# Four experts for each of 32 tokens in a gather, four column groups of TensorE, and a ring of four slots

## The chip, the cores and the metric

The kernel runs on one core of a Trainium2 chip. The metric is the time of one execution on the device, in microseconds (us); lower is better. TensorE is written PE here, its weight loads PEld, VectorE DVE, ScalarE ACT, GpSimd POOL and SyncE SP. A name with a q behind it (POOLq) is an engine's sequencer. "Line 1757" or L1757 is a line of the kernel before; lines of the changed kernel are called so.

## What is computed

One step of a decoder layer: two mixers (an S5 scan and a Mamba-2 scan), a residual, and a channel mixer of single-neuron experts (PEER). The change touches the channel mixer alone. For each of 1088 tokens (1024 of a prompt, 64 sampled) it chooses 8 x 16 = 128 of 16384 experts, and adds up their value rows, each with the gelu of its key row's product with the token:

```python
def peer_ffn(h, w_q, sub_keys, u_tab, v_tab):
    q = (xt @ w_q).astype(F32).reshape(T, PEER_HEADS, 2, PEER_HALF)
    s = jnp.einsum('thid,hikd->thik', q, sub_keys.astype(F32))
    sv, si = lax.top_k(s, PEER_TOPK)
    cand = sv[:, :, 0, :, None] + sv[:, :, 1, None, :]
    cv, cpos = lax.top_k(cand.reshape(T, PEER_HEADS, PEER_TOPK * PEER_TOPK), PEER_TOPK)
...
    idx = i1 * PEER_N_KEYS + i2
    g = jax.nn.softmax(cv, axis=-1)
...
        u = u_tab[ib]
        act = jax.nn.gelu(jnp.einsum('thkd,td->thk', u, xb).astype(F32))
        v = v_tab[ib]
        return jnp.einsum('thk,thkd->td', (gb * act).astype(v.dtype), v)
```

The input xb is the token after an RMSNorm; the sum is added to the residual x, and a last RMSNorm gives the output y. All is 32-bit float, and a row of u or v has 1024 elements. In the kernel's table `uv` the two rows of an expert stand side by side, so one row of it has 8 KB.

## The kernel before

The function `route_and_experts` is the last stage. It works on nine tiles of tokens: eight main tiles of 128 tokens, one turn each of a hardware loop (`Fori(0, MAIN_TILES)`, on every engine), and a last tile of the 64 sampled tokens, written out behind the loop. Within a turn everything is unrolled.

**Gathers.** A main tile has 128 gathers, one for each of a token's 128 experts: gather g brings, for each of the 128 tokens (one to a partition), the row `uv` of its g-th expert, so 128 rows of 8 KB. POOL issues it as one indirect DMA (line 1576) into one slot of `ring`, which has RING = 8 slots. It may do so when the slot's last user is through: `group_done`, raised by PE. The sample tile folds its 64 tokens over 128 partitions (`folded`, three small DMAs), two experts at a time, and has 64 gathers.

**One gather's work** runs through four engines:

- DVE (line 1757) multiplies the u half of the slot by the token rows `h_now` and sums along the row: one dot product for each partition.
- ACT (line 1617) takes the gelu of the 128 dot products.
- DVE (line 1745, `weigh`) makes `diag`, a 128x128 diagonal matrix of gelu times gate. It stands one gather late in DVE's order: behind the dot product of g comes weigh(g - 1).
- PE (line 1832) multiplies `diag` by the v half of the slot, as two matmuls of 512 columns, each of which is two passes in the trace (four records a gather, since the data is fp32), and adds into the PSUM tensor `acc`. Its last matmul raises `group_done`, and POOL issues gather g + 8 into the slot.

**Routing** of the next tile is done meanwhile, in 64 steps (ROUTE_STEPS), one behind every second gather (EVERY = 2), on ACT, DVE and PE, in an order written out by hand: the norm of x, transposes of h (line 1793), the query matmuls (16 steps, line 1803, 16 records each), scores (line 1813), top-k steps on DVE (lines 1658 to 1731, some of them over 2048 elements a partition: lines 1640 and 1722), and a softmax. `index` and `gate` are its results. POOL copies the index to `index_now` (lines 1565 and 1580).

**The end of a tile.** Behind the last gather PE adds x (line 1819); ACT sums the squares (line 1621), loads a function table and takes the root (line 1623), and copies x to `x_now`; DVE takes the reciprocal (line 1766) and writes `out` (line 1768); SP stores it (line 1536) and loads the next x (line 1532). Then every engine branches back to the loop's top, where DVE copies `gate_now` and `h_now` (lines 1749 and 1750) before its first dot product. PE's first `add_x` waits for `x_now` and for `out`.

## Time and profile before

| | us |
|---|---|
| three runs | 4724.04, 4724.33, 4729.05 |
| median | 4724.33 |
| span of the profiled execution | 4728.8 |
| busy in it: PE, DVE, POOL, ACT | 3724.3, 2737.7, 1485.7, 691.1 |
| bytes moved by the gathers' queue | 1140.92 MB |

The last stage starts its gathers at about 1891 us and runs to the end, so it holds six tenths of the time, and all that the change touches. The busy shares of the whole span (PE 79%, DVE 58%, POOL 31%, ACT 15%) mix it with the stages ahead of it and are of little use; the stage is read by windows, by the distance of repeated instructions, and by the chain of waits.

### The profile page before, as it was taken

How to read it: one execution, taken by the hardware profiler on the slowest of the kernel's cores; microseconds unless marked ns; L12 is line 12 of the kernel's file. 1: busy time of each engine (PE TensorE's matmuls, PEld its weight loads, DVE VectorE, ACT ScalarE, POOL GpSimd, SP SyncE). 2: the span in 40 equal slices, each digit the busy share in tenths (PEclk: the TensorE clock that was granted, in tenths of full speed). 3: DMA queues.
4: the chain of work that ended last, by engine and by line, in shares of the span. 5: the costliest groups of instructions: out<-in, count | busy, mean ns of one | idle time of the engine just before them, and what ended most of it. 6: DMA issues, size and time to landing. Idle time of an engine off the chain costs nothing.

```text
span 4728.8 us, 44920 instructions
## 1 busy us (share of the span) xinstructions
PE 3724.3 (79%) x12914; PEld 1960.8 (41%) x12914; DVE 2737.7 (58%) x5963; ACT 691.1 (15%) x1844; POOL 1485.7 (31%) x1547
## 2 busy tenths in 40 slices
PE   8999590745469994887977978978878879779777
PEld 5767460723334443432532523534424325325221
DVE  1000529158831114687686785785886876867865
ACT  1110120112223220101101111111111011011110
POOL 3000310401100000444444443454444444444442
PEclk9999755867679997999999999999999999999999
DMA  4111300121131112999999999999999999999998
GB/s 161 61 40 36 75 2 2 47 95 41 34 152 67 54 44 105 411 412 395 413 418 390 415 419 393 412 421 394 416 419 394 416 413 392 415 389 414 420 401 360
DMA packets 253462, 1271.34 MB, mean 269 GB/s; under 512 B 62096, under 2 KB 92432, under 8 KB 113168
## 3 DMA queue, kind: packets, MB, share of 16 engines
q0 software_dynamic: 156672, 1140.92, 58.6%
q1 hardware_dynamic: 96576, 127.93, 8.1%
q8 instruction: 90, 1.47, 0.1%
q14 instruction: 124, 1.02, 0.1%
HBM read 1226.22 MB, written 40.09 MB: 268 GB/s over the span
## 4 chain that ended last, share of the span: by engine, by line
DMA 23%; PE 21%; DVE 8%; issue 7%; POOL 2%; ACT 0%; POOLq 0%; DVEq 0%; SPq 0%; ACTq 0%
DMA pe_ring<-in_uv,pe_index_now 20%; PE pe_acc L1832 15%; PE pe_ps_q L1803 5%; DVE pe_ring L1757 2%; DMA pe_ring<-in_uv,pe_index 2%; POOL pe_ring L1576 2%; DVE pe_work_a L1640 2%; DVE pe_diag L1745 1%; DVE pe_picked L1722 1%; PE pe_ps_s L1813 1%; PE pe_acc L1819 0%; DMA pe_w_q<-in_w_q 0%; DVE pe_top L1699 0%; ACT pe_square L1621 0%; DVE pe_dot L1757 0%
## 5 line engine op out<-in xcount | busy, mean ns | idle before, releaser
L1832 PE MATMUL pe_acc<-pe_ring,pe_diag 128*128 128x512 f32 (+1 forms) x4352 | 2069.4, 618 | 451.7 <-DVE pe_diag L1745 451.1
L1576 POOL DMA_INDIRECT pe_ring<-in_uv,pe_index_now x1024 | 1211.9, 1184 | 1304.8 <-PE pe_acc L1832 1120.5
L1757 DVE CUSTOM_DVE_ANT_0 pe_ring<-pe_ring,pe_h_now 128x1024 f32<-128x1024 f32 x1024 | 1252.7, 1224 | 553.4 <-DMA pe_ring<-in_uv,pe_index_now 550.7
L1832 PEld LDWEIGHTS pe_acc<-pe_ring,pe_diag 128*128 128x128 f32 (+1 forms) x4352 | 786.6, 192 | 1636.7 <-DVE pe_diag L1745 908.2
L1617 ACT ACTIVATE pe_act_v<-pe_dot 128x1 f32<-128x1 f32 x1088 | 220.6, 203 | 2395.1 <-DVE pe_dot L1757 2390.2
L1745 DVE TENSOR_SCALAR pe_diag<-pe_ident,pe_act_v,pe_gate_now 128x128 f32<-128x128 f32 x1024 | 355.3, 347 | 56.3 <-DVE pe_top L1686 7.4
L1803 PEld LDWEIGHTS pe_ps_q<-pe_h_t,pe_w_q 128*128 128x128 f32 x2304 | 280.7, 194 | 63.8 <-issue 61.2
L1803 PE MATMUL pe_ps_q<-pe_h_t,pe_w_q 128*128 128x128 f32 x2304 | 281.5, 277 | 2.2 <-DMA pe_w_q<-in_w_q 2.2
L372 PE MATMUL pj_bank<-pj_w_in,pj_normed_t 128*128 128x512 f32 (+1 forms) x720 | 267.7, 529 | 5.6 <-DMA pj_w_in<-in_w_in 5.6
L1392 PE MATMUL mo_ps_out<-mo_w_out,mo_both_t 128*128 128x512 f32 x576 | 251.2, 594 | 14.7 <-DVE mo_both_t L1342 11.9
L378 PE MATMUL pj_bank<-pj_normed_t,pj_w_in 128*128 128x128 f32 x1728 | 195.2, 276 | 0.0
L378 PEld LDWEIGHTS pj_bank<-pj_normed_t,pj_w_in 128*128 128x128 f32 x1728 | 193.7, 192 | 0.0
L372 PEld LDWEIGHTS pj_bank<-pj_w_in,pj_normed_t 128*128 128x128 f32 x720 | 126.6, 192 | 141.2 <-issue 141.2
L1580 POOL COPY pe_index_now<-pe_index 128x64 int32<-128x64 int32 x1 | 0.2, 236 | 567.2 <-DVE pe_index L1728 567.2
L1392 PEld LDWEIGHTS mo_ps_out<-mo_w_out,mo_both_t 128*128 128x128 f32 x576 | 108.7, 190 | 150.5 <-issue 136.5
L954 PE MATMUL m2p_a<-m2s_x_dt,m2s_decay 128*128 128x64 f32 x288 | 63.5, 422 | 106.7 <-DVE m2s_decay L850 106.7
L440 POOL MEMSET s5s_b_apart<- 128x512 f32 x1 | 0.5, 524 | 426.6 <-POOLq L108 426.6
L1392 PE MATMUL mo_ps_glu<-mo_w_glu,mo_g_t 128*128 128x512 f32 x288 | 127.9, 603 | 1.9 <-ACT mo_g_t L1323 1.9
L314 DVE COPY pj_chan_out<-pj_bank 128x512 f32<-128x512 f32 x18 | 12.5, 692 | 192.0 <-PE pj_bank L378 192.0
L777 PE MATMUL s5p_u_psum<-s5s_ident,s5s_u_rest 128*128 128x128 f32 x64 | 12.5, 278 | 136.3 <-POOL s5s_u_rest L735 136.3
L1757 DVE CUSTOM_DVE_ANT_0 pe_ring<-pe_ring,pe_h 128x1024 f32<-128x1024 f32 x64 | 78.3, 1225 | 61.7 <-DMA pe_ring<-in_uv,pe_index 61.7
L954 PEld LDWEIGHTS m2p_a<-m2s_x_dt,m2s_decay 128*128 128x128 f32 x288 | 61.8, 331 | 114.1 <-DVE m2s_decay L850 114.1
(302 smaller groups left out, 3083.0 us busy)
## 6 DMA issues: line engine op xcount, KB each, us to landing
pe_ring<-in_uv,pe_index_now POOLq DMA_INDIRECT x1024
pe_w_q<-in_w_q SPq DMA_DIRECT2D x4, 2048.0 KB, 19.9
m2s_window<-scratch_xbc SPq DMA_DIRECT2D x8, 786.0 KB, 5.1
pj_w_in<-in_w_in SPq DMA_DIRECT2D x1, 6144.0 KB, 38.6
scratch_xbc<-pj_chan_out SPq DMA_DIRECT2D x8, 768.0 KB, 5.1
pj_x<-in_x_all SPq DMA_DIRECT2D x9, 512.0 KB, 4.7
scratch_u<-pj_token_out SPq DMA_DIRECT2D x9, 512.0 KB, 2.6
scratch_z<-pj_token_out SPq DMA_DIRECT2D x9, 512.0 KB, 3.7
```

What stands on the lines that cost most here:

```text
L372: last = nc.tensor.matmul(b[:, 0:w], x_t[:, k, :], w_in[:, k, a:a + w], start=k == 0, stop=k == KT - 1)
L378: last = nc.tensor.matmul(b[:, c * P:(c + 1) * P], w_in[:, k, a:a + P], x_t[:, k, :], start=k == 0, stop=k == KT - 1)
L954: last = nc.tensor.matmul(ps_a[:, h // HPG, (h % HPG) * HD:(h % HPG + 1) * HD], decay[:, h, :], x_dt[:, h, :], start=True, stop=True)
L1392: last = T.matmul(flat(dst)[:, half * 512:half * 512 + 512], src_t[:, c, :], w[:, c, half * 512:half * 512 + 512], start=first and c == c0 ...
L1576: nc.gpsimd.indirect_dma_start(out=ring[:, s, :], out_offset=None, in_=D["uv"], in_offset=bass.IndirectOffsetOnAxis(ap=row, axis=0)).then_ ...
L1617: A(act_v[:, cols], dot[:, cols], ACT.Gelu_apprx_tanh).then_inc(act_ready, 1)
L1640: tt = lambda o, a, b, op: V.tensor_tensor(out=o, in0=a, in1=b, op=op)
L1722: chain.link(V.tensor_reduce(out=picked[:, b, :], in_=hit, axis=AX.X, op=ALU.add))
L1745: last = V.tensor_scalar(diag[:, s, 0:width], eye[:], act_v[:, s:s + 1], gates[:, col:col + 1], ALU.mult, ALU.mult)
L1757: last = V.tensor_tensor_reduce(out=ring[:, s, 0:D_MODEL], in0=ring[:, s, 0:D_MODEL], in1=tokens[:], scale=1.0, scalar=0.0, op0=ALU.mult, ...
L1803: last = T.matmul(ps_q[:, n % 2, j % UNIT, :], w_q[:, c, j * P:(j + 1) * P], h_t[:, c, :], start=c == 0, stop=c == KT - 1)
L1832: last = T.matmul(acc[0:width, b, :], diag[:, s, 0:width], ring[:, s, D_MODEL + b * 512:D_MODEL + b * 512 + 512], start=False, stop=False)
```

## The change

**A gather** now holds four experts for each of 32 tokens: partition j * 32 + t belongs to token t of the group and to an expert of quarter j of its 128. A main tile is 4 groups (GROUPS) of 32 operations (PER), so still 128 gathers of 128 rows; the sample tile is 2 groups of 32. For this `index` and `gate` are transposed: two PE transposes and a DVE transpose at routing step CHOICE, in a new order of the two results (gate first).

**Tokens** are repeated over the four quarters of the partitions: `repeat` (PE, two matmuls of 512 columns with `pick`) makes the rows and ACT copies them to `h_rep`, once for each group, at operations 16 and 20 of the group ahead of it.

**The weights** are made by ACT in two instructions of 128x32: `mark` is the gelu of a repeated 32x32 identity times the dot product, and `weight` is `mark` times the gate. DVE's `weigh` is gone.

**PE** multiplies `weight` (128 rows, 32 columns) by the v half in four matmuls of 256 columns (`quarters`), quarter j of the columns into partitions 32 j to 32 j + 31 of `acc`. A group is finished (sum of squares on ACT, sum of the four parts on PE, root on ACT, `out` on DVE) at operations 1, 2, 4 and 6 of the next group, in the other half of `acc`; the last group of a tile is finished behind its last operation, before the branch. `out` is 128x256, stored in four DMAs of 32 rows of 1 KB.

**The ring** has four slots in place of eight: `op_done`, raised by `quarters`, lets POOL issue gather n + 4. The `folded` DMAs are gone.

The diff, cut to its core; runs of unchanged or renamed lines are left out:

```diff
-    RING, GROUP = 8, 1
+    RING = 4
+    GROUPS, PER = 4, 32
+    COLS = D_MODEL // GROUPS
...
+    CHOICE = SUMS + 22
+    assert CHOICE + 1 < (OPS - RING) // EVERY - 2
+    REP, REP_COPY, NOW_COPY = 16, 20, 14
...
+        mark = sb("mark", [P, RING, PER])
+        weight = sb("weight", [P, RING, PER])
+        h_rep = sb("h_rep", [P, 2, D_MODEL])
...
+            def store(k, g):
+                sp.wait_ge(y_ready, GROUPS * k + g + 3)
+                for j in range(GROUPS):
+                    sp.dma_start(D["y"][bass.ds(k * P + g * PER, PER), j * COLS:(j + 1) * COLS],
+                                 out[j * PER:(j + 1) * PER, g % 2, :]).then_inc(y_out[g % 2], 16)
...
+            def copy_rep(n, g):
+                act.wait_ge(rep_made, n)
+                A(h_rep[:, g % 2, :], ps_t[:].rearrange("p c n -> p (c n)"), ACT.Copy).then_inc(rep_ready, 1)
+            def sum_squares(k, g):
+                act.wait_ge(op_done, k * OPS + g * PER + PER + RING)
+                A(acc[:, g % 2, COLS:2 * COLS], acc[:, g % 2, 0:COLS], ACT.Square, accum_out=end_stat[:, g % 2, 0:1]).then_inc(part_summed, 1)
+            def take_root(k, g):
+                act.wait_ge(end_summed, GROUPS * k + g + 1)
+                A(end_stat[:, g % 2, 1:2], acc[:, g % 2, COLS:COLS + 1], ACT.Sqrt, bias=eps[:], scale=1.0 / D_MODEL).then_inc(end_root, 1)
             def tile(k, groups, more):
-                for g in range(groups):
-                    p, slots, use = place(g)
-                    cols = slice(slots[0], slots[-1] + 1)
-                    act.wait_ge(dots_ready, k * GROUPS + g + 1)
-                    A(act_v[:, cols], dot[:, cols], ACT.Gelu_apprx_tanh).then_inc(act_ready, 1)
-                    if more and g % EVERY == EVERY - 1:
-                        route(k + 1, g // EVERY)
-                act.wait_ge(tile_done, k + 1)
-                A(square[:], acc[:].rearrange("p b c -> p (b c)"), ACT.Square, accum_out=end_stat[:, 0:1]).then_inc(end_summed, 1)
-                act.wait_ge(end_summed, k + 1)
-                A(end_stat[:, 1:2], end_stat[:, 0:1], ACT.Sqrt, bias=eps[:], scale=1.0 / D_MODEL).then_inc(end_root, 1)
-                if more:
-                    A(x_now[:], x[:], ACT.Copy).then_inc(x_now_ready, 1)
+                act.wait_ge(index_ready, k + 1)
+                A(gate_now[:], choice[:, 1, :], ACT.Copy).then_inc(gate_now_ready, 1)
+                act.wait_ge(gate_now_ready, k + 1)
+                for n in range(groups * PER):
+                    g, s, p = n // PER, n % PER, n % RING
+                    act.wait_ge(dots_ready, k * OPS + n + 1)
+                    A(mark[:, p, :], eye[:], ACT.Gelu_apprx_tanh, scale=dot[:, p:p + 1]).then_inc(mark_ready, 1)
+                    act.wait_ge(mark_ready, k * OPS + n + 1)
+                    A(weight[:, p, :], mark[:, p, :], ACT.Copy, scale=gate_now[:, n:n + 1]).then_inc(weight_ready, 1)
+                    if g and s == 1:
+                        sum_squares(k, g - 1)
+                    if g and s == 4:
+                        take_root(k, g - 1)
+                    if s == NOW_COPY and g == GROUPS - 1 and more:
+                        act.wait_ge(seeded, GROUPS * k + GROUPS)
+                        act.wait_ge(rep_made, GROUPS * k + GROUPS)
+                        copy_now()
+                    if s == REP_COPY and (more or g + 1 < groups):
+                        copy_rep(GROUPS * k + g + 2, g + 1)
+                    if more and n % EVERY == EVERY - 1:
+                        route(k + 1, n // EVERY)
+                sum_squares(k, groups - 1)
+                take_root(k, groups - 1)
...
+                if g == CHOICE + 1:
+                    dve.wait_ge(choice_turned, r + 1)
+                    if more:
+                        dve.wait_ge(gate_now_ready, r)
+                    chain.link(V.transpose(choice[:], ps_q[:, 0, 0:2, :]))
+                    if more:
+                        dve.wait_ge(index_taken, 2 * r)
+                    V.tensor_copy(index[:], choice[:, 0, :]).then_inc(index_ready, 1)
+            def finish(k, g):
+                dve.wait_ge(end_root, GROUPS * k + g + 1)
+                end.link(V.reciprocal(end_stat[:, g % 2, 2:3], end_stat[:, g % 2, 1:2]))
+                dve.wait_ge(y_out[g % 2], 64 * (2 * k + g // 2) + 64)
+                V.scalar_tensor_tensor(out=out[:, g % 2, :], in0=acc[:, g % 2, 0:COLS], scalar=end_stat[:, g % 2, 2:3], in1=final_w[:],
+                                       op0=ALU.mult, op1=ALU.mult).then_inc(y_ready, 1)
...
-                def weigh(g):
-                    dve.wait_ge(act_ready, k * GROUPS + g + 1)
-                    for s in place(g)[1]:
-                        col = g * GROUP + s % GROUP
-                        last = V.tensor_scalar(diag[:, s, 0:width], eye[:], act_v[:, s:s + 1], gates[:, col:col + 1], ALU.mult, ALU.mult)
-                    last.then_inc(diag_ready, 1)
...
+                for n in range(groups * PER):
+                    g, s, p = n // PER, n % PER, n % RING
+                    if s == 0:
+                        dve.wait_ge(rep_ready, GROUPS * k + g + 1)
+                    dve.wait_ge(rows_in[p], 16 * (k * USES + n // RING + 1))
+                    V.tensor_tensor_reduce(out=ring[:, p, 0:D_MODEL], in0=ring[:, p, 0:D_MODEL], in1=h_rep[:, g % 2, :],
+                                           scale=1.0, scalar=0.0, op0=ALU.mult, op1=ALU.add, accum_out=dot[:, p:p + 1]).then_inc(dots_ready, 1)
+                    if g and s == 6:
+                        finish(k, g - 1)
+                    if more and n % EVERY == EVERY - 1:
+                        route(k + 1, n // EVERY, True)
+                finish(k, groups - 1)
+                assert end.n == groups
...
+                if g == CHOICE:
+                    pe.wait_ge(choice_ready, 2 * r + 2)
+                    T.transpose(ps_q[:, 0, 0, :], pos_f[:, 0, :], ident[:])
+                    T.transpose(ps_q[:, 0, 1, :], gate[:].rearrange("p h c -> p (h c)"), ident[:]).then_inc(choice_turned, 1)
+            def repeat(g):
                 for b in range(2):
+                    last = T.matmul(ps_t[:, 4 * b:4 * b + 4, :].rearrange("p c n -> p (c n)"), pick[:, g].rearrange("p q t -> p (q t)"),
+                                    h_now[:, b * 512:b * 512 + 512], start=True, stop=True)
+                last.then_inc(rep_made, 1)
+            def quarters(lhs, src, g, first, final):
+                for j in range(GROUPS):
+                    last = T.matmul(acc[j * PER:(j + 1) * PER, g % 2, 0:COLS], lhs(j), src[:, j * COLS:(j + 1) * COLS], start=first, stop=final)
                 return last
+            def add_parts(k, g):
+                pe.wait_ge(part_summed, GROUPS * k + g + 1)
+                T.matmul(acc[:, g % 2, COLS:COLS + 1], same[:].rearrange("p q t -> p (q t)"), end_stat[:, g % 2, 0:1],
+                         start=True, stop=True).then_inc(end_summed, 1)
             def tile(k, groups, more):
+                for n in range(groups * PER):
+                    g, s, p = n // PER, n % PER, n % RING
+                    if s == 0:
+                        if g == 0:
+                            pe.wait_ge(x_now_ready, k + 1)
+                        pe.wait_ge(y_ready, GROUPS * k + g + 1)
+                        quarters(lambda j: pick[:, g, j, :], x_now, g, True, False).then_inc(seeded, 1)
+                    pe.wait_ge(weight_ready, k * OPS + n + 1)
+                    quarters(lambda j: weight[:, p, :], ring[:, p, D_MODEL:], g, False, s == PER - 1).then_inc(op_done, 1)
+                    if g and s == 2:
+                        add_parts(k, g - 1)
+                    if s == REP and (more or g + 1 < groups):
+                        if g == 0 and more:
+                            pe.wait_ge(h_t_ready, k + 2)
+                        else:
+                            pe.wait_ge(rep_ready, GROUPS * k + g + 1)
+                        if g == GROUPS - 1:
+                            pe.wait_ge(h_now_ready, k + 2)
+                        repeat((g + 1) % GROUPS)
+                    if more and n % EVERY == EVERY - 1:
+                        route(k + 1, n // EVERY, True)
+                add_parts(k, groups - 1)
...
-                for g in range(groups):
-                    p, slots, use = place(g)
-                    pe.wait_ge(diag_ready, k * GROUPS + g + 1)
-                    for s in slots:
-                        for b in range(2):
-                            last = T.matmul(acc[0:width, b, :], diag[:, s, 0:width], ring[:, s, D_MODEL + b * 512:D_MODEL + b * 512 + 512],
-                                            start=False, stop=False)
-                    last.then_inc(group_done, 1)
-                    if more and g % EVERY == EVERY - 1:
-                        route(k + 1, g // EVERY)
-                add_x(1).then_inc(tile_done, 1)
```

How the instructions stand now, at three places. PE in the loop, around two of the query steps of a tile; before (`pe_ps_q` takes the queries of the next tile, `pe_acc` the sums of this one):

```order
L1832 MATMUL pe_acc<-pe_ring,pe_diag 128x512 x2
L1829 REGISTER_ALU
L1832 MATMUL pe_acc<-pe_ring,pe_diag 128x512 x2
L1803 MATMUL pe_ps_q<-pe_h_t,pe_w_q 128x128 x8
L1829 REGISTER_ALU
L1832 MATMUL pe_acc<-pe_ring,pe_diag 128x512 x2
```

and after:

```order
L1858 MATMUL pe_acc<-pe_ring,pe_weight 32x256 x4
L1851 MATMUL pe_ps_t<-pe_h_now,pe_pick 128x512 x2
L1875 REGISTER_ALU
L1858 MATMUL pe_acc<-pe_ring,pe_weight 32x256 x4
L1831 MATMUL pe_ps_q<-pe_h_t,pe_w_q 128x128 x8
L1875 REGISTER_ALU
L1858 MATMUL pe_acc<-pe_ring,pe_weight 32x256 x4
```

The two matmuls of a gather have become four with a quarter of the output rows and half of the columns, and `repeat` stands between two of them. ACT at the end of a main tile and the top of the next, before:

```order
L1617 ACTIVATE pe_act_v<-pe_dot 128x1
L1621 ACTIVATE pe_square,pe_end_stat<-pe_acc 128x1024
L1623 ACT_TABLE_LOAD
L1623 ACTIVATE pe_end_stat<-pe_end_stat,pe_eps 128x1
L1625 ACTIVATE pe_x_now<-pe_x 128x1024
L1631 REGISTER_ALU
L1631 COMPARE_AND_BRANCH
```

and after:

```order
L1629 ACTIVATE pe_mark<-pe_eye,pe_dot 128x32
L1631 ACTIVATE pe_weight<-pe_mark,pe_gate_now 128x32
L1615 REGISTER_ALU
L1616 ACTIVATE pe_acc,pe_end_stat<-pe_acc 128x256
L1620 ACT_TABLE_LOAD
L1620 ACTIVATE pe_end_stat<-pe_acc,pe_eps 128x1
L1653 REGISTER_ALU
L1653 COMPARE_AND_BRANCH
```

The copy of x is gone from here (it stands in the last group now), and each operation has two ACT instructions. At its loop's top the changed ACT has a table load, the copy of the gates, and a second table load. DVE at the same place, before:

```order
L1745 TENSOR_SCALAR pe_diag<-pe_ident,pe_act_v,pe_gate_now 128x128
L1766 RECIPROCAL pe_end_stat<-pe_end_stat 128x1
L76 REGISTER_ALU
L1768 SCALAR_TENSOR_TENSOR pe_out<-pe_acc,pe_end_stat,pe_final_w 128x1024
L1780 REGISTER_ALU
L1780 COMPARE_AND_BRANCH
```

and after:

```order
L1781 ISA pe_dot 128x1
L1767 RECIPROCAL pe_end_stat<-pe_end_stat 128x1
L1769 SCALAR_TENSOR_TENSOR pe_out<-pe_acc,pe_end_stat,pe_final_w 128x256
L1804 REGISTER_ALU
L1804 COMPARE_AND_BRANCH
```

The last `out` of a tile still stands ahead of DVE's branch, and the next tile's first dot product behind it.

## Rows read from the trace of the kernel before

**Rows 1.** The page, busy tenths of the span in 40 slices:

```profile
PEclk9999755867679997999999999999999999999999
DMA  4111300121131112999999999999999999999998
```

**Rows 2.** Windows: stretch, its length, busy us (x instructions), clock, DMA share, GB/s:

```profile
core 0: us, PE busy (x) PEld busy (x) DVE busy (x) ACT busy (x) POOL busy (x), PEclk, DMA share, GB/s
600.00:700.00 100.00, 97.58 (x425) 62.77 (x421) 20.46 (x47) 21.17 (x94) 21.39 (x69) 0.50 0.03 2
...
2237.00:2247.00 10.00, 8.13 (x15) 3.61 (x16) 10.00 (x23) 1.42 (x7) 2.95 (x4) 0.74 0.43 148
...
4600.00:4700.00 100.00, 76.80 (x160) 18.40 (x158) 58.43 (x120) 8.06 (x40) 38.20 (x40) 1.00 1.01 421
```

**Rows 3.** One line's instructions, L1565, the copy ahead of a tile's eighth gather:

```profile
L1565 POOL COPY pe_index_now<-pe_index x8: 233/290/757, 1906.3 to 4238.6; 128x64 int32<-128x64 int32 x8
```

**Rows 4.** Chain of waits, one turn of the ring: start us, us, what:

```profile
4648.14 13.12 DMA pe_ring<-in_uv,pe_index
...
4662.80 1.95 PE pe_acc L1832 x4
...
4665.54 13.13 DMA pe_ring<-in_uv,pe_index
```

**Rows 5.** Timeline, the same stretch: start us, us, engine, line, [idle before <-releaser]:

```profile
4658.80 1.23 DVE L1757 CUSTOM_DVE_ANT_0 pe_ring<-pe_ring,pe_h 128x1024 f32<-128x1024 f32 x1 [1.02 <-DMA pe_ring<-in_uv,pe_index]
...
4660.07 0.20 ACT L1617 ACTIVATE pe_act_v<-pe_dot 128x1 f32<-128x1 f32 x1 [2.28 <-DVE pe_dot L1757]
...
4665.54 0.94 POOL L1576 DMA_INDIRECT pe_ring<-in_uv,pe_index  x1 [1.55 <-PE pe_acc L1832]
```

**Rows 6.** Timeline at a tile boundary, first gather that misses its queue, and its dot product:

```profile
2243.66 1.33 POOL L1576 DMA_INDIRECT pe_ring<-in_uv,pe_index_now  x1 [0.81 <-POOL pe_index_now L1565]
...
2249.58 1.23 DVE L1757 CUSTOM_DVE_ANT_0 pe_ring<-pe_ring,pe_h_now 128x1024 f32<-128x1024 f32 x1 [2.35 <-DMA pe_ring<-in_uv,pe_index_now]
```

**Rows 7.** Timeline, the stretch of PE with two column groups, and serial matmuls:

```profile
615.65 1.21 PE L600 MATMUL s5p_y_psum<-s5s_toep,s5s_u_t 128*128 x4
616.79 1.19 PE L607 MATMUL s5p_v_psum<-s5s_u_t,s5s_in_t 128*64 128x138 f32 x8
...
1805.13 1.94 PE L1793 MATMUL pe_ps_t<-pe_ident,pe_h 128*128 128x128 f32 x8 [17.87 <-DVE pe_h L1650]
```

**Rows 8.** Timeline from the last dot product of a tile to the next tile's first work:

```profile
2212.71 1.46 POOL L1576 DMA_INDIRECT pe_ring<-in_uv,pe_index_now  x1 [5.24 <-issue]
...
2219.58 1.23 DVE L1757 CUSTOM_DVE_ANT_0 pe_ring<-pe_ring,pe_h_now 128x1024 f32<-128x1024 f32 x1 [0.99 <-DMA pe_ring<-in_uv,pe_index_now]
...
2227.71 1.28 ACT L1623 ACT_TABLE_LOAD   x1
...
2229.21 1.04 ACT L1625 ACTIVATE pe_x_now<-pe_x 128x1024 f32<-128x1024 f32 x1
...
2229.53 1.28 DVE L1768 SCALAR_TENSOR_TENSOR pe_out<-pe_acc,pe_end_stat,pe_final_w 128x1024 f32<-128x1024 f32 x1
...
2235.16 0.23 DVE L1749 COPY pe_gate_now<-pe_gate 128x128 f32<-128x128 f32 x1 [4.34 <-issue]
```

**Rows 9.** Timeline, a long DVE step and the POOL issue under it:

```profile
2478.41 2.71 POOL L1576 DMA_INDIRECT pe_ring<-in_uv,pe_index_now  x1 [2.51 <-PE pe_acc L1832]
...
2478.03 2.29 DVE L1640 TENSOR_TENSOR pe_work_a<-pe_work_a,pe_best_f 128x2048 f32<-128x2048 f32 x1
```

**Rows 10.** Groups by shape, one tile (2235 to 2567 us): busy us, mean ns:

```profile
L1576 POOL DMA_INDIRECT pe_ring<-in_uv,pe_index_now x128 | 150.7, 1177 | 164.3 <-PE pe_acc L1832 142.2 <-issue 20.5 <-POOL pe_index_now L1565 0.8
...
L1617 ACT ACT_TABLE_LOAD x3 | 3.8, 1283 | 0.1
```

**Rows 11.** Timeline, PE at one query step, the engine behind its work:

```profile
3003.89 1.95 PE L1803 MATMUL pe_ps_q<-pe_h_t,pe_w_q 128*128 128x128 f32 x16
...
3009.11 1.95 PE L1803 MATMUL pe_ps_q<-pe_h_t,pe_w_q 128*128 128x128 f32 x16
```

191 lines of the change are left out of this document (83 added, 108 removed).

## The prediction

> **What bounds the kernel now.** I read the page's slices first, then windows of the last stage, then the distance of repeated instructions, then the chain of waits through one turn of the ring. In the slices the DMA engines are at 9 tenths from about 1890 us to the end and mostly idle before, and TensorE's clock stays at 9 there [rows 1]. In the window 4600 to 4700 all DMA engines are busy (1.01), at 421 GB/s and clock 1.00, though PE is busy for 77 us of 100 [rows 2]. So the stage is bound by the gathers' bytes. The chain gives the cadence: from 4648.14 to 4665.54, one turn of the ring, are 17.40 us, in which seven gathers land [rows 4], C = 2.485 us each. A main tile would be 128 x 2.485 = 318.1 us; the same copy at eight successive tiles, 1906.3 to 4238.6, says 2332.3 / 7 = 333.2 [rows 3]. The difference, 15.1 us a tile and 121 in all (2.6%), is what a change that leaves the bytes alone can win. One piece of it can be seen: the queue runs dry at a tile boundary. Dot product 127 starts at 2219.58 [rows 8]; dot product 8 of the next tile, whose gather was issued too late, at 2249.58 [rows 6]: 30.0 us for nine gathers worth 22.4, so 7.6 late. The other 7.5 us come from work around the gathers.
>
> The bytes stay the same, so I count what keeps the queue fed: a slot's turn against the turn that the ring allows.
>
> **The ring.** Eight slots allow 8 x 2.485 = 19.9 us, four allow 9.94. What a turn needs, into an empty queue:
>
> - PE's end to POOL's issue .80 (4662.80 + 1.95 to 4665.54) [rows 4], the issue .94 [rows 5];
> - its end to the dot product 4.59 (2243.66 + 1.33 to 2249.58) [rows 6];
> - dot product to ACT 1.27 (4658.80 to 4660.07) [rows 5];
> - two ACT instructions of 128x32. None is in the trace: a 128x1 takes .20 [rows 5], a 128x1024 1.04 [rows 8]; near the first, .24 each, and .05 to PE.
>
> That is 8.13, and PE's operation comes on top.
>
> **PE's four matmuls** are 256 columns each in two passes. Side by side they last two steps, one after another eight. The only column groups in the trace are L607's, eight records of 64 output columns by 138: 1.19 us [rows 7], with the clock at .50 there, 1.2 GHz [rows 2]. L1793's eight records of 128, serial, take 1.94 [rows 7], just under .25 each with the fill. So two groups do run side by side: 4 steps of .23 and a fill of .27. With four groups I take 2 steps of .43 (a 512-column pass takes .43 at 2.4 GHz, four of them 1.73 of the 1.95 of [rows 4]; 256 columns at half the clock the same) and .27: **1.12 us** at 1.2 GHz and .69 at 2.4 GHz. The bounds are pairs (1.98 and 1.11) and serial work (3.6 and 1.95). PE's array work falls from 1.73 to .43 us a gather (both at 2.4 GHz), and in the stretch of short narrow matmuls the clock is .50 [rows 2], so I expect the lower clock for about half of the stage. The turn needs 8.13 + 1.12 = 9.25 of 9.94: the cadence holds, with **.7 us of room** (1.1 at the full clock), where eight slots leave some ten.
>
> The rows of L600 and L607 overlap by .07 us, though their shapes differ [rows 7], so I price a change of shape at nothing. "TensorEngine Tiling (Array Packing)" of the Trainium skill, section Key Properties, says that a change of tiling mode drains the array. By that, with the fill of .27 as an estimate of a drain, 16 query steps with two changes each would add 8.6 us a tile to the sum below.
>
> **What exceeds the room, R.** Each delay within a turn now counts beyond .7:
>
> - POOL's issue is stretched under long DVE steps: 2.71 us beside 2.29 us of DVE on 2048 elements [rows 9]. A tile has seven such steps (lines 1640 and 1722, and the sums): 7 x (2.71 - .94 - .70) = 7.5. Smaller stretches (the mean issue is 1.18 [rows 10]) another 1.5.
> - ACT's table loads, 1.28 [rows 10]. Root or Exp, with a load before and one behind, is 2.86, against 2.485 - .48 = 2.0 free: with the 1024-wide square of the next tile, 2.4 in all.
> - PE's query steps. A pair of gathers with one takes 5.2 us now (3003.89 to 3009.11) [rows 11], more than 4.97. After, at the full clock, 1.95 + 2 x .69 = 3.3; at the lower 3.4 + 2.24 = 5.6, .6 too much, 16 times: 9 if the clock is low throughout, 4.4 at half.
> - `repeat`, 3.4 at the lower clock in a gap of 1.36: 1.3 beyond the room, four times, half of the time: 2.6.
>
> R = 18.4 us a tile. Bounds: 8 (POOL's alone) and 28 (low clock throughout).
>
> **The tile boundary**, from the start of dot product 127: ACT 1.27, PE starts at 1.80 and ends at 2.92, ACT's square of 256 columns to 3.5, from the table load's start to `out` 1.82 (2227.71 to 2229.53) [rows 8], so `out` at 5.3. From `out` to DVE's next instruction are 5.63 us (2229.53 to 2235.16), of which 4.34 wait for nothing that the profile shows, behind the branch; POOL has such a wait of 5.24 [rows 8]. Next dot product at 11.05, ACT 12.3, weight 12.8, PE to 13.97, POOL's index copy 1.04 (2242.62 to 2243.66, the .23 copy and .81 idle [rows 6]), issue at 15.1 to 16.1, and 4.59 later, at 20.7, dot product 4. Five gathers are worth 12.4: **8.3 us late**, beside 7.6 before. DVE's wait stays on the path and the shorter ring takes back what the shorter end gives. ACT has two table loads and a copy at its loop's top; if its body, half as long again as before, now waits at the branch too, it is ready at 12.1 to 13, so 0 to .7 more.
>
> "Runtime: NRT & Kernel Launch" of the Trainium skill, section Instruction fetch mechanics, says that a taken branch whose target is outside the two fetched pages waits for a fetch. DVE's and POOL's rows agree with it [rows 8].
>
> **Small terms.** x's load, in a window where 148 GB/s are moved [rows 2], and y's store: 2.5 us a tile; 1 KB rows in place of 4 KB .3. Two transposes and a DVE step ahead of the first gather +1.5 once. At the very end `out` is a quarter as wide and no x is added: -4 once. Taking `weigh` from DVE is worth nothing, since DVE waits for DMA (1.02 us in each cadence [rows 5]); without that cover it would be .24 a gather, what 2.485 leaves beside 1.23 and 1.02.
>
> **The sum.** 318.1 + 2.5 + .3 + 8.3 + 18.4 = 347.6 us a tile, +14.4 on 333.2, eight times +115; with +1.5 and -4, +112.7: 4728.8 + 112.7 = 4841.5 for a run like the profiled one. The median is 4.5 lower than that span: 4837.
>
> **The rivals.**
>
> *Absorbed.* With the clock high (query steps free, room 1.1) and delays that fall into one turn counted once, R is 5: 318.1 + 2.8 + 8.3 + 5 = 334.2, +8 - 2.5: 4730, between 4715 and 4755. For it: the tile of before loses only 7.5 us outside its boundary. Against it: it had ten us of cover.
>
> *Faster.* One place, DVE's wait behind the branch. DVE's body loses 128 `weigh` with their register instructions; if it no longer waits there, dot product 0 starts at 6.3, the boundary costs 3.6, and with R = 5 the tile is 329.5: -3.7 x 8 - 2.5 = -32: 4692. It decides at boundary + R = 12.6. For it: the changed ACT and DVE bodies differ, and ACT's short one had no such wait. Against: POOL, whose body is shorter than DVE's, has it in full, and R is small only at the high clock.
>
> *The column groups do not run side by side*, or only in pairs at the lower clock; the change would not do what it says. The turn is 8.13 + 1.95 = 10.08, above 9.94: 2.52 a gather, 322.6 a tile, and no delay has any room. Seven DVE steps at 1.77 and 1.5 make 14, ACT 5, query pairs 16 x (5.85 - 5.04) = 13, `repeat` 5; with 2.8 and a boundary of 9.4 that is 372: +39 x 8: 5030, between 4950 and 5100. L607's row speaks against it for two groups; none shows four.
>
> **How the numbers follow.** The forecast (4750 to 4920 by the bounds of R) .60; absorbed .10; faster .15; no side by side .15. A range from 4700 to 4990 leaves out about .1 at the faster end and .08 at the other. A measurement of this kernel can tell .2% from no change, 9.4 us: within it .07, half and more of the absorbed case; faster by more .16; slower by more .77.
>
> **What would show it.** The POOL copy of eight successive tiles 347 us apart; dot products 2.485 apart where nothing disturbs (2.52 or more: the third rival); PE's operation 1.1 or .7 long; the granted clock of the stage below 1; late dot products four gathers behind a 2048-element DVE step; 20.7 us from dot product 127 to dot product 4. A clock that stays high, or a turn well under 9.2, would leave R near 8 or less and make the forecast too slow.

## The result

The changed kernel takes 5210.16 us in the median (5206.42 to 5229.95) against 4724.34 before: a ratio of 1.1033, with an interval from 1.1013 to 1.1053. It is slower by 10%, the way that was forecast, but 373 us above the forecast and 220 above the range.

The page of the changed kernel, clock, DMA share and rate in 40 slices:

```profile
PEclk9998657767899967557557558557557557557555
DMA  4111101211311349999999999999999999999998
GB/s 155 47 50 68 20 3 22 101 33 41 158 47 54 111 168 349 343 339 345 348 334 356 346 347 358 359 335 348 348 343 357 350 334 350 346 346 354 355 350 352
```

The DMA row hardly differs from [rows 1]: the engines are at 9 tenths. But the rate beside it is some 350 GB/s, where the kernel before has 389 to 421 in the stage's slices but the last. Here lies the whole result: engines that look as busy bring a seventh less. The same window of the stage, in the kernel before and in the changed one (its length, busy us of PE, PEld, DVE, ACT, POOL, clock, DMA share, GB/s) answers to [rows 2]:

```profile
3000.00:3400.00 400.00, 342.34 (x1030) 164.10 (x1028) 300.65 (x782) 51.31 (x183) 187.15 (x159) 0.97 0.99 409
```

```profile
3000.00:3400.00 400.00, 188.37 (x1418) 74.68 (x1418) 223.05 (x490) 116.88 (x311) 152.32 (x137) 0.62 0.94 356
```

The rate falls from 409 to 356 GB/s, the share only from .99 to .94. PE's busy time has fallen from 342 us to 188, and DVE's from 301 to 223. No engine has become the bound. The copy ahead of a tile's next slot, as in [rows 3]:

```profile
L1561 POOL COPY pe_index_now<-pe_index x8: 250/334/1027, 1901.4 to 4640.9; 128x64 int32<-128x64 int32 x8
```

2739.5 / 7 = 391.4 us a tile, where 347.6 was forecast. Counted from a tile's first dot product to the next tile's, the seven main tiles behind the first take 389.3 us each in the mean, against 332.1 before. The rest of this text uses that count.

The chain of waits of the changed kernel in its sample tile, where no routing runs, answers to [rows 4]:

```profile
5145.36 6.00 DMA pe_ring<-in_uv,pe_index_now
...
5151.39 1.23 DVE pe_ring L1781
...
5152.66 0.33 ACT pe_mark L1629
5153.01 0.33 ACT pe_weight L1631
...
5153.39 1.12 PE pe_acc L1858 x8
...
5155.31 6.92 DMA pe_ring<-in_uv,pe_index_now
...
5162.25 1.22 DVE pe_ring L1781
```

One turn is 5145.36 to 5155.31, 9.95 us. The parts that the prediction built up are there: 1.27 to ACT, PE's 1.12, the issue. Two are longer: .33 for an ACT instruction in place of .24, and 6.0 from the issue to the dot product, in place of 5.53. This last one must be read with care. Where the gathers land at their cadence, a turn of four slots lasts 4 x 2.485 = 9.94 us whatever it needs, and time that it has over is spent waiting behind the gather before. Dot product to issue is 3.92 here, so 6.02 are left for the rest by this sum alone. In the next turn the same piece takes 6.92, and in the two after it 8.51 and 6.01, with nothing else at work.

The boundary of a tile, in the timeline of the changed kernel, answers to [rows 6, 8]:

```profile
2282.28 1.23 DVE L1781 CUSTOM_DVE_ANT_0 pe_ring<-pe_ring,pe_h_rep 128x1024 f32<-128x1024 f32 x1 [1.77 <-DMA pe_ring<-in_uv,pe_index_now]
...
2287.70 0.48 DVE L1769 SCALAR_TENSOR_TENSOR pe_out<-pe_acc,pe_end_stat,pe_final_w 128x256 f32<-128x256 f32 x1
...
2291.86 1.28 ACT L1624 ACT_TABLE_LOAD   x1 [4.39 <-issue]
...
2293.50 1.23 DVE L1781 CUSTOM_DVE_ANT_0 pe_ring<-pe_ring,pe_h_rep 128x1024 f32<-128x1024 f32 x1 [5.32 <-issue]
...
2297.93 1.11 POOL L1570 DMA_INDIRECT pe_ring<-in_uv,pe_index_now  x1 [0.81 <-PE pe_acc L1858]
...
2303.54 1.23 DVE L1781 CUSTOM_DVE_ANT_0 pe_ring<-pe_ring,pe_h_rep 128x1024 f32<-128x1024 f32 x1 [5.33 <-DMA pe_ring<-in_uv,pe_index_now]
```

From dot product 127 (2282.28) to dot product 4 of the next tile (2303.54) are 21.3 us; 20.7 were forecast. ACT now waits 4.39 us behind its branch, which it did not before. The gather issued at 2297.93 finds the queue empty, and from its issue to its dot product are 5.61 us; the shortest of the main tiles behind the first is 5.46. So a turn at rest needs 3.92 and some 5.5, which is 9.4 to 9.5 us: some .4 to .5 us of the forecast's .7 us of room are there.

### The profile page after: what moved, and what is told of

Same layout as the page of the kernel before. It is cut to its first block, busy times and chain, and to the rows that moved or that the text cites. A ratio compares the mean times of both kernels' runs of the same rounds, so it can differ in the third digit from the quotient of the medians.

```text
span 5204.6 us, 54439 instructions
## 1 busy us (share of the span) xinstructions
PE 2933.2 (56%) x17688; PEld 1506.1 (29%) x17688; DVE 2467.3 (47%) x4924; ACT 1292.4 (25%) x3117; POOL 1456.1 (28%) x1547
## 4 chain that ended last, share of the span: by engine, by line
DMA 36%; issue 9%; PE 8%; DVE 6%; ACT 5%; POOL 1%; POOLq 0%; SPq 0%; DVEq 0%; ACTq 0%
DMA pe_ring<-in_uv,pe_index_now 36%; PE pe_acc L1858 6%; DVE pe_ring L1781 4%; PE pe_ps_q L1831 2%; ACT pe_mark L1629 2%; ACT pe_weight L1631 2%; PE pe_ps_t L1851 1%; POOL pe_ring L1570 1%; DVE pe_work_a L1662 1%; ACT L1629 1%; ACT L1620 0%; DVE pe_dot L1781 0%; DMA pe_w_q<-in_w_q 0%; DVE pe_picked L1745 0%; DVE pe_pos L1727 0%
## 5 line engine op out<-in xcount | busy, mean ns | idle before, releaser
L1781 DVE CUSTOM_DVE_ANT_0 pe_ring<-pe_ring,pe_h_rep 128x1024 f32<-128x1024 f32 x1088 | 1332.1, 1226 | 1482.0 <-DMA pe_ring<-in_uv,pe_index_now 1425.4
L1858 PE MATMUL pe_acc<-pe_ring,pe_weight 128*32 128x256 f32 x8704 | 1050.1, 574 | 1693.6 <-ACT pe_weight L1631 1674.2
L1570 POOL DMA_INDIRECT pe_ring<-in_uv,pe_index_now x1088 | 1241.0, 1141 | 1966.2 <-PE pe_acc L1858 1825.0
L1858 PEld LDWEIGHTS pe_acc<-pe_ring,pe_weight 128*32 128x32 f32 x8704 | 211.5, 133 | 2463.4 <-ACT pe_weight L1631 2388.1
L1629 ACT ACTIVATE pe_mark<-pe_eye,pe_dot 128x32 f32<-128x32 f32 x1088 | 349.5, 321 | 2266.1 <-DVE pe_dot L1781 2258.8
L1831 PE MATMUL pe_ps_q<-pe_h_t,pe_w_q 128*128 128x128 f32 x2304 | 356.9, 320 | 3.1 <-DMA pe_w_q<-in_w_q 3.1
L1631 ACT ACTIVATE pe_weight<-pe_mark,pe_gate_now 128x32 f32<-128x32 f32 x1088 | 349.5, 321 | 35.1
L1831 PEld LDWEIGHTS pe_ps_q<-pe_h_t,pe_w_q 128*128 128x128 f32 x2304 | 329.5, 229 | 68.0 <-issue 64.6
L1851 PE MATMUL pe_ps_t<-pe_h_now,pe_pick 128*128 128x512 f32 x136 | 109.2, 949 | 0.0
L850 POOL TENSOR_TENSOR m2s_da_upto<-m2s_da,m2s_upto 128x2048 f32<-128x2048 f32 x8 | 28.9, 3609 | 249.2 <-DVE m2s_da L850 249.2
```

Source lines behind the costliest of these rows:

```text
L1570: nc.gpsimd.indirect_dma_start(out=ring[:, p, :], out_offset=None, in_=D["uv"], in_offset=bass.IndirectOffsetOnAxis(ap=row, axis=0)).then_ ...
L1629: A(mark[:, p, :], eye[:], ACT.Gelu_apprx_tanh, scale=dot[:, p:p + 1]).then_inc(mark_ready, 1)
L1631: A(weight[:, p, :], mark[:, p, :], ACT.Copy, scale=gate_now[:, n:n + 1]).then_inc(weight_ready, 1)
L1781: V.tensor_tensor_reduce(out=ring[:, p, 0:D_MODEL], in0=ring[:, p, 0:D_MODEL], in1=h_rep[:, g % 2, :], scale=1.0, scalar=0.0, op0=ALU.mult ...
L1831: last = T.matmul(ps_q[:, n % 2, j % UNIT, :], w_q[:, c, j * P:(j + 1) * P], h_t[:, c, :], start=c == 0, stop=c == KT - 1)
L1851: last = T.matmul(ps_t[:, 4 * b:4 * b + 4, :].rearrange("p c n -> p (c n)"), pick[:, g].rearrange("p q t -> p (q t)"), h_now[:, b * 512:b ...
```

## The experiments

Three readings stood against each other. **Room** ("turn" in the first expectations): a turn needs all of the 9.94 us, and each delay of the tile's other work counts in full; some us more would heal it. (By the boundary's row above a little room is there, .4 to .5 us; the expectations take it as none.) **Layout**: a gather of four experts for 32 tokens is in itself slower than one of one expert for 128. **Shallow queue**: the DMA engines slow down when few gathers are issued and not yet landed, also without a delay from elsewhere. The packets' records of the changed kernel gave rise to the last two: between 2300 and 3400 us a packet of 8 KB takes .350 us in the mean instead of .317, and 6.7% of them take over .5 us, instead of .7%. The median packet is no slower (.309 us, .312 before); all of it is in the long ones, and five in six of them stand in the first and last quarter of a gather.

### The depth of the ring

Eight slots in the changed kernel:

```diff
-    RING = 4
+    RING = 8
```

> The changed kernel with eight slots in place of four; nothing else is changed. Theory 'turn': in the changed kernel's trace a slot's turn is 3.92 us from dot product to the next issue and 6.02 from the issue to the dot product where nothing disturbs, 9.94 in all, exactly the 4 x 2.485 that four slots allow; every disturbance then lets the DMA queues run dry. With eight slots there are ten us of room, so the tile falls from 389 us to about 330 (318.1 + 2.8 + a boundary of 4 + 5): 4690 to 4740 us, at or below the kernel before. Theory 'layout': the gather of four experts for 32 tokens is itself slower in the DMA engines (a packet takes .356 us on the mean instead of .317): then eight slots change little, 5050 to 5200 us, and packets stay at .35.

4684.02 us, .9907 of the kernel before (.9890 to .9923): faster than the changed kernel by a tenth, and than the kernel before by .9%. Its window:

```profile
3000.00:3400.00 400.00, 211.74 (x1649) 81.54 (x1648) 264.50 (x619) 137.23 (x367) 177.34 (x159) 0.64 1.00 415
```

The layout, the column groups, ACT's two instructions and the low clock (.64) are all still there, and the rate is 415 GB/s. So with eight slots these cost nothing; the packets are back at .315 us. Without the shorter ring nothing of the 10% is left. With eight slots POOL was then held to a depth of five and of six:

```diff
-            pool.sem_inc(op_done, RING)
+            pool.sem_inc(op_done, DEPTH)
...
-                act.wait_ge(op_done, k * OPS + g * PER + PER + RING)
+                act.wait_ge(op_done, k * OPS + g * PER + PER + DEPTH)
```

> The changed kernel with eight slots, of which POOL uses a depth of five: gather n waits for operation n - 5. It separates two readings of the 9.94 us. Theory 'room': a turn needs 9.94, so five slots have 2.5 us of room, more than any single delay of the tile but the boundary's; main tiles of 330 to 340 us, 4750 to 4830 in all. Theory 'shallow queue': what counts is how many gathers' work the DMA engines have before them; in the changed kernel 7% of the packets last over .5 us (mean .35) because at most one more gather is issued behind the one that is read, against .4 to .7% (mean .315) where two or three are. Then the gain grows step by step with the depth: 12.4 - 4.9 us are left for the DMA, 3.0 gathers instead of 2.0, tiles of 345 to 365 us, 4880 to 5020, long packets 2 to 4%.

4787.25 us (ratio 1.0128), 339.7 us a tile, 1.9% of the packets long. The time lies in the range of "room"; the share of long packets lies just under that of "shallow queue", whose curve I had drawn too flat. By itself this run speaks for "room".

> The same with a depth of six. 'Room': as with eight but for the boundary, 328 to 333 us a tile, 4700 to 4750. 'Shallow queue': 4.0 gathers before the DMA engines, most of the loss gone: 332 to 342 us a tile, 4740 to 4840, long packets near 1%.

4690.39 us (.9923), 327.6 a tile, .6% long: almost as good as eight, better than either expected, and nearer to "room". The curve is steep and ends at six. What "room" can't have is a loss where there is room or no disturbance, and that is what the next runs look for.

### The same turn, shorter, with four slots

Two more matmuls keep PE at the full clock:

```diff
+                    if 3 <= s < PER - 1:
+                        for b in range(2):
+                            T.matmul(acc[:, g % 2, COLS + 1:2 * COLS], ident[:], w_q[:, b, 0:COLS - 1], start=False, stop=False)
```

> The changed kernel with two more matmuls of 128 rows by 255 columns behind the four of operations 3 to 30 of each group, into the unused half of acc; they add nothing to the result. They keep TensorE busy, so that it gets its full clock: an operation's four matmuls should take .69 us instead of 1.12. Theory 'turn': .43 us of room instead of none, worth some 2 to 3 of the 10 us that eight slots give, and query steps no longer beyond the cadence: 5000 to 5120 us. Theory 'layout': no change beyond 1%, 5160 to 5220.

5195.32 us (1.0987). The clock rose and PE's part fell as meant:

```profile
3000.00:3400.00 400.00, 286.53 (x1878) 155.93 (x1876) 217.71 (x487) 118.11 (x311) 153.06 (x135) 0.86 0.94 350
```

From dot product to the next issue the median is 3.49 us instead of 3.92, and the tile is 389.4 us, the same. But the mean, over gathers 6 to 121 of the third tile, only falls from 4.11 to 3.94, and what the turn gives off there, the DMA's piece takes: issue to dot product grows from 7.93 to 8.10. "Room" expected 90 us or more, six times what came. The forecast gave the low clock a share of R, and no such share shows here, though the added matmuls keep PE busy as well and so blur the test.

One ACT instruction instead of two:

```diff
-                    A(mark[:, p, :], eye[:], ACT.Gelu_apprx_tanh, scale=dot[:, p:p + 1]).then_inc(mark_ready, 1)
-                    act.wait_ge(mark_ready, k * OPS + n + 1)
-                    A(weight[:, p, :], mark[:, p, :], ACT.Copy, scale=gate_now[:, n:n + 1]).then_inc(weight_ready, 1)
+                    A(weight[:, p, :], eye[:], ACT.Gelu_apprx_tanh, scale=dot[:, p:p + 1]).then_inc(weight_ready, 1)
```

> The changed kernel with one ACT instruction for each gather in place of two: the gate is left out of the weights (that part of the result is missing). Theory 'turn': .35 us of room instead of none, at the lower clock: 5030 to 5140 us, a little less gained than by the full clock, since query steps stay slow. Theory 'layout': no change, 5160 to 5220.

5153.72 us (1.0899), 383.7 a tile: between the two expectations, 14 us above "turn" and 6 below "layout". This edit adds no work. Over the same gathers the mean from dot product to issue falls by .37 us, to 3.74, and issue to dot product grows by .30, from 7.93 to 8.23. Most of what the turn gives off is taken back before the gather lands. Both edits together:

> The changed kernel with one ACT instruction for each gather and the two extra matmuls that keep TensorE at its full clock: .78 us less in the turn in all. The gate is missing from the weights. Each alone gained 57 and 15 us. 'Shallow queue', with 5.9 us left to the DMA engines: between the changed kernel (5.1 us, 389 us a tile) and the one with early release (6.6 us, 355): 370 to 380, 5040 to 5110. If the extra matmuls themselves cost something elsewhere, no better than one ACT instruction alone, 5140 to 5160.

5141.00 us (1.0871), 382.6 a tile: 31 us above the range that I had for "shallow queue", and next to one ACT instruction alone, as the last sentence of the expectation has it. In the mean, dot product to issue is 3.68 us there, against 3.74 with one ACT instruction alone and 4.11 in the changed kernel: of the .78 that I took from the steady turn, .43 arrives. That the extra matmuls delay others often enough to eat their own gain is a guess from these means.

A larger step: the slot is released as soon as ACT has the dot products, and PE reads a constant. Left out below: ACT now waits itself for PE's end of the operation four before, so that no weight is overwritten too soon.

```diff
-                    quarters(lambda j: weight[:, p, :], ring[:, p, D_MODEL:], g, False, s == PER - 1).then_inc(op_done, 1)
+                    quarters(lambda j: weight[:, p, :], w_q[:, 0, 0:D_MODEL], g, False, s == PER - 1).then_inc(op_done, 1)
...
-                    pool.wait_ge(op_done, k * OPS + n + 1)
+                    pool.wait_ge(mark_ready, k * OPS + n + 1)
```

> The changed kernel with its four slots, but PE's four matmuls read a constant tensor in place of the slot, and POOL issues the next gather into a slot as soon as ACT has its dot products (the value rows' part of the result is wrong by that). It takes the weight and PE, 1.5 us, out of the turn and leaves the number of slots. 'Room': 1.5 us of room, most delays are covered: 335 to 350 us a tile, 4790 to 4910. 'Shallow queue': 6.6 us or 2.7 gathers are left to the DMA, between the changed kernel and a depth of five: 355 to 375 us a tile, 4950 to 5100. That taking .35 or .43 us out of the turn gained 57 and 15 us speaks for the second.

4914.73 us (1.0397), 355.0 a tile, 3.6% long packets. It lies between the two: 5 us above the ranges of "room", and 35 us in time below that of "shallow queue", at whose near end the tile is. With 1.5 us of room 23 us a tile are still lost against the kernel before, twice what the routing will turn out to cost at no room at all. The window shows it without a waiting engine to blame:

```profile
3000.00:3400.00 400.00, 213.66 (x1598) 92.70 (x1598) 231.91 (x507) 125.83 (x335) 153.07 (x146) 0.63 0.97 380
```

### Without the tile's other work

All routing steps are taken out of the loop, on ACT, DVE and PE (DVE shown), with the waits for their results.

```diff
-                    if more and n % EVERY == EVERY - 1:
-                        route(k + 1, n // EVERY, True)
```

> The changed kernel without the 64 routing steps inside the loop (every main tile uses the first tile's experts, so the output is wrong): no long DVE steps, no query matmuls, no root or Exp of the routing. It sizes the term R of the prediction by itself. By the prediction (R = 18.4 of a tile, the rest sound) a tile would be 330 to 335 us, 4740 to 4770 with the lost R read as 389 - 332 = 57. Theory 'shallow queue': the sample tile of the changed kernel, which has no routing, already needs 2.81 us a gather, so 128 x 2.81 + a boundary of 5: 360 to 368 us a tile, 4960 to 5030.

5099.14 us (1.0783), 377.7 a tile. This is the measurement of R, but for `repeat` (2.6 of the forecast's 18.4), which the run keeps: the routing costs 389.3 - 377.7 = 11.6 us a tile with four slots. The time is 330 us above "room" and 69 above "shallow queue": I had taken the 2.81 us a gather of a stretch of the sample tile, and the main tile's mean is 2.92.

```profile
3000.00:3400.00 400.00, 163.47 (x1154) 35.50 (x1146) 169.93 (x280) 108.96 (x303) 142.63 (x140) 0.52 0.94 361
```

ACT is busy for 109 us of 400, PE for 163, DVE for 170, and the engines bring 361 GB/s. The 46 us a tile above the kernel before are there with no disturbance from routing. This run, more than the others, takes "room" out as it was put, with the tile's other work as what disturbs. What it leaves in is the scatter of the gathers themselves, which the open points below take up.

### The old layout with four slots

The kernel before, with four slots:

```diff
-    RING, GROUP = 8, 1
+    RING, GROUP = 4, 1
```

> The kernel before with four slots in place of eight; nothing else is changed. Theory 'turn': dot product to PE 1.52, PE 1.95, to POOL .80, issue to dot product 6.02: 10.29 of 9.94 us, so 2.57 a gather at best, 329 us a tile, and each disturbance counts in full, a little worse than the changed kernel: 5200 to 5350 us. Theory 'layout': four slots cost little with the old layout, 4730 to 4850 us, packets at .32.

6261.84 us (1.3242), 515 a tile, some thousand us more than "turn" expected. I had overlooked what the description of the kernel before states: weigh(g - 1) stands behind dot product g, so PE's work on a slot waits for the next gather to land, and of four slots three are left to the DMA. With that put right:

```diff
                     last.then_inc(dots_ready, 1)
+                    weigh(g)
                     if more and g % EVERY == EVERY - 1:
                         route(k + 1, g // EVERY, True)
-                    if g:
-                        weigh(g - 1)
-                weigh(groups - 1)
```

> The kernel before with four slots, and weigh(g) moved directly behind dot product g. In the kernel before it stands behind the next dot product, so a slot is held for one gather more; with four slots that made 6262 us (515 us a tile). This is the fair test of four slots with the old layout (128 tokens, one expert). Turn outside the DMA: dot product to PE 1.27 + .2 + .3, PE 1.95, POOL .80 + .94, 5.5 us, against 4.9 in the changed kernel. Theory 'shallow queue': 4.5 us left to the DMA engines against 5.1: worse than the changed kernel, 410 to 440 us a tile, 5350 to 5600 us. Theory 'layout' (a gather of four experts for 32 tokens is slower in itself): about as before with small losses, under 4900.

5476.58 us (1.1581), 419.7 a tile, 7.9% long packets, in the range of "shallow queue". The old layout loses in the same way, and more, with its longer turn (4.93 us from dot product to issue in the median, against 3.92), so "layout" falls from this side too. The windows of the two:

```profile
3000.00:3400.00 400.00, 264.22 (x691) 118.44 (x692) 204.65 (x512) 27.24 (x112) 113.56 (x101) 0.87 0.75 264
```

```profile
3000.00:3400.00 400.00, 292.62 (x794) 127.70 (x792) 251.17 (x561) 41.45 (x146) 140.09 (x124) 0.94 0.88 324
```

### All of them on one line

For each kernel: outstanding is the mean time from a gather's issue to its dot product, divided by the mean distance of dot products (gathers 262 to 377, inside the third tile); it is measured, not set. Packets are those of 8 KB between 2300 and 3400 us. The last two kernels are told of in the next section.

| kernel | us | us a tile | outstanding | mean packet us | over .5 us |
|---|---|---|---|---|---|
| before, four slots | 6262 | 514.7 | 1.6 | .367 | 10.4% |
| before, four slots, weigh at once | 5477 | 419.7 | 2.4 | .356 | 7.9% |
| changed | 5210 | 389.3 | 2.6 | .350 | 6.7% |
| changed, no routing | 5099 | 377.7 | 2.6 | .343 | 5.6% |
| changed, full clock | 5195 | 389.4 | 2.7 | .352 | 7.0% |
| changed, one ACT instruction | 5154 | 383.7 | 2.8 | .348 | 6.1% |
| changed, both | 5141 | 382.6 | 2.8 | .350 | 6.5% |
| changed, early release | 4915 | 355.0 | 3.1 | .333 | 3.6% |
| changed, depth five | 4787 | 339.7 | 3.4 | .322 | 1.9% |
| changed, depth six | 4690 | 327.6 | 4.3 | .316 | .6% |
| changed, eight slots | 4684 | 326.7 | 6.3 | .315 | .4% |
| before | 4724 | 332.1 | 4.6 | .317 | .7% |
| before, weigh at once | 4729 | 331.7 | 5.6 | .317 | .7% |
| changed, eight slots, end put off | 4684 | 327.1 | 6.3 | .316 | .6% |

Over the whole table time falls as the outstanding gathers rise, whatever set them: slots, depth, release or layout. Within the five kernels at 2.6 to 2.8 the order is not kept (the one without routing has 2.6 and is the fastest of them), and from 4.3 up more of them bring no more. Between 4.3 and 3.4 the loss begins, and part of it shows as longer packets. Over five tiles (the third to the seventh) of the changed kernel, the packets of all queues take 363.4 us a tile of each engine's time (329.5 before) and 26.4 are idle (3.2 before). So of 57 us, 34 are longer packets and 23 are engines with nothing to read.

### Where the gain of eight slots comes from

Two tries to explain and to extend the 44 us by which the changed kernel with eight slots beats the kernel before (4728.2 us, timed along with it). The first moves weigh(g) forward as above, with eight slots.

> The kernel before with its eight slots and weigh(g) directly behind dot product g. It asks where the 44 us come from that the changed kernel with eight slots gains on the kernel before. If from the slot held one gather longer: 4690 to 4710 us. If from DVE's end of the tile (out four times as wide and x added behind the last gather) and from PE and DVE being less busy: DVE now waits for ACT at every gather as well, 4715 to 4750.

4728.93 us, a ratio of 1.0001 (.9992 to 1.0011): no change, so the late weigh is not it. The second finishes the last group of a tile in the next tile and writes the first tile out ahead of the loop:

```diff
-                    if g and s == 6:
-                        finish(k, g - 1)
+                    if s == 6 and not (first and g == 0):
+                        finish(*ahead(k, g))
...
-                finish(k, groups - 1)
+                if not more:
+                    finish(k, groups - 1)
```

> The changed kernel with eight slots, and the last group of each tile finished within the first group of the next (ACT, PE and DVE at its operations 1, 2, 4 and 6, as the other groups), so that nothing stands between the last dot product and the branch; the first tile is written out ahead of the loop, which has seven turns. With eight slots alone a tile takes 327.5 us, of which one gap of 7 to 8 us between gathers 7 and 8 (5 more than the cadence) is the boundary's. DVE branches 4 us earlier, so that gap should shrink by about 4: 323.5 us a tile, 7 times, 4684 - 28 = 4656 us. Rival: POOL's or ACT's own wait behind the branch takes the place of DVE's; then half or less, 4670 to 4684.

4683.62 us (.9910; .9894 to .9927), the same as without it. That is the edge of the rival's range, but the boundary did shrink, by more than the expectation's 4 us. DVE from dot product 127 to the next, with eight slots alone and with the end put off:

```profile
3200.63 1.22 DVE L1781 CUSTOM_DVE_ANT_0 pe_ring<-pe_ring,pe_h_rep 128x1024 f32<-128x1024 f32 x1 [1.26 <-DMA pe_ring<-in_uv,pe_index_now]
...
3211.96 1.23 DVE L1781 CUSTOM_DVE_ANT_0 pe_ring<-pe_ring,pe_h_rep 128x1024 f32<-128x1024 f32 x1 [5.42 <-issue]
```

```profile
3197.59 1.23 DVE L1792 CUSTOM_DVE_ANT_0 pe_ring<-pe_ring,pe_h_rep 128x1024 f32<-128x1024 f32 x1 [1.24 <-DMA pe_ring<-in_uv,pe_index_now]
...
3203.34 1.23 DVE L1792 CUSTOM_DVE_ANT_0 pe_ring<-pe_ring,pe_h_rep 128x1024 f32<-128x1024 f32 x1 [4.52 <-issue]
```

11.3 us have become 5.8, and the gap in the gathers (from the first packet of one to that of the next) falls from some 7 to 8 us to 3 to 5, but the tile stays at 327. The reason that the trace offers is that the packets' time of all queues is already the whole tile: 328.2 us of 327.5 with eight slots, 330.0 of 327.6 with the end put off (records overlap a little, hence the excess). In the kernel before it is 329.5 of 332.7. The 5 us a tile that eight slots win are then idle time of the DMA engines and a little packet time, and no more is to be had from the boundary. Which part of the change wins them was not isolated.

## Why the prediction was wrong, step by step

- **The bound**, gathers' bytes at 2.485 us each, was right for eight slots.
- **PE's four matmuls** side by side, 1.12 us at 1.2 GHz: 1.12 in the chain. Right, and the third rival fell (its 5030 is nearer to the measured time than the forecast's 4837, by luck); the clock is .50 in the sample tile (.62 in the window above, with routing).
- **The boundary**: 20.7 us forecast, 21.3 measured, 8.8 late instead of 8.3. Right. That ACT might pay behind its branch too was foreseen as 0 to .7 us more, and it does, with 4.39 us of idle time. "Runtime: NRT & Kernel Launch" of the Trainium skill, section Instruction fetch mechanics, says that a taken branch waits for a fetch when its target is not among the two pages at hand. The trace agrees: ACT's turn of the loop has 448 recorded instructions now, 287 before, and only the longer one waits.
- **The turn**: 9.25 us forecast into an empty queue, 9.4 to 9.5 measured: 3.92 from dot product to issue (3.72 forecast; .18 of the difference is ACT's, .33 an instruction) and 5.46 to 5.61 from there to the dot product (5.53 forecast). Right within .3 us. The 9.94 us that the expectations take for the need of a turn is the cadence itself. A room of some .4 to .5 us was there, and did not keep the cadence.
- **R**, the tile's disturbances: 18.4 forecast, of which 15.8 without `repeat`; 11.6 measured for these. A share of the clock in it was not seen: with the clock up, and the matmuls for it added, the tile is the same.
- **The step that failed** is the sentence "the cadence holds, with .7 us of room". It treats the DMA engines as a server that gives a gather every 2.485 us as long as a turn fits into four of them. That figure was measured with more than four gathers outstanding, and I carried it over to 2.6. With the measured terms, 318.1 + 2.8 + 8.8 + 11.6 = 341.3 us; the tile takes 389.3. The missing 48 us are this step's, more than twice what boundary and routing cost together.
- The reasoning on the rivals asked where a delay lands, never whether the bound itself moves with the queue's depth. "Absorbed" and "faster" describe the kernel with eight slots, where the tile came to 326.7, below the faster rival's 329.5. Its mechanism was another: DVE waits behind its branch as before (5.42 us of idle time).

**Open**: why a packet takes longer when few gathers are outstanding. That the long ones stand at the ends of a gather suggests an engine that has no next request at hand, but it was not shown. Within the kernel before, gathers with three others issued behind them (at the start of their 97th packet) have .1% of long packets, those with two .8% and those with one 2.4%. Within the changed kernel it is not so: none behind 5.6%, one 6.8%, two 8.8%. So the depth at the moment is not all of it. A rival was not tested either: that the gathers' own scatter is the disturbance that "room" lacked. A gather is through with its last packet. From the start of a gather's first packet to the end of its last (128 of them in order of start, gathers 262 to 377) are 3.59 us in the median in the changed kernel and 2.79 in the kernel before, at the shortest 2.76 and 2.74. It may be that one engine or another lags, that with a short ring the others run dry until it is through, and that a deep ring gives them the next gather meanwhile. Both accounts make the ring's depth the cause. That the full clock, with the matmuls that bring it, leaves the tile as it was is shown; that these ate the gain is only argued from the means.

## What to carry to other kernels

Before a ring is shortened, take the bytes' rate at the depth that it will have, not at the one that it has: the cadence of a transfer-bound stage is a measurement at one depth. A turn that just fits was already too long here. A depth of six in place of four was worth 520 us and a release 1.5 us earlier 295; an ACT instruction less and PE's full clock, together, were worth 69. And read GB/s next to the DMA share: .94 with 356 GB/s and 1.00 with 415 look alike in tenths.

## What the hardware showed

- Random rows of 8 KB, 128 in a gather: 415 GB/s with 6.3 gathers outstanding, 412 with 4.3, 402 with 3.4, 380 with 3.1, 356 with 2.6, 324 with 2.4, 264 with 1.6 (window 3000 to 3400 us; outstanding as in the table).
- The median 8 KB packet is .309 to .312 us with 2.6 gathers outstanding and with 4.6; the 95th of a hundred goes from .319 to .602.
- Four column groups of 256 columns, two passes each, take 1.12 us at the clock .50; eight such passes one after another would be 3.4, an estimate by the .43 of the prediction.
- An ACT instruction over 128x32 takes .32 us, against .20 over 128x1.
- Taking 5.5 us (11.3 to 5.8, from dot product 127 to the next) out of each tile boundary gave nothing with eight slots, where the packets' records already fill the tile (328.2 us of 327.5).
